# Two of three weight sums of a seven-product unit on GpSimd instead of VectorE, and the work at four pass ends placed anew

## The reference

```python
h2 = rms_norm(x, norm2_g[l])
ff = jnp.square(jax.nn.relu(h2 @ w_ff1[l]))      # 256 x 8192
x = x + ff @ w_ff2[l]                            # 8192 x 2048, the "down" product
return rms_norm(x, final_g)                      # then the third block, built alike:
x = x + jnp.square(jax.nn.relu(h @ w_up[l])) @ w_down[l]
return rmsnorm(x, norm_final_g)
```

## Time and profile before

| | |
|---|---|
| median of 3 runs | 3254.99 us (3254.61 to 3255.85) |
| profiled execution, own time | 3254.65 us |
| its span | 3252.9 us |
| TensorE busy | 3223.1 us, 99% |
| VectorE busy | 2388.0 us, 73% |
| ScalarE busy | 1593.2 us, 49% |
| GpSimd busy | 350.9 us, 11% |
| granted TensorE clock | 0.999 of full speed |

### The profile page before, as it was taken

One profiled execution on the slowest core, in us unless ns is written; L12 is line 12 of the kernel. 1 busy time (PEld: TensorE's weight loads), 2 busy tenths in 40 slices (PEclk: granted clock), 3 DMA queues, 4 the chain that ended last, 5 costly groups with the idle time before them and its releaser, 6 DMA issues.

```text
span 3252.9 us, 51117 instructions
## 1 busy us (share of the span) xinstructions
PE 3223.1 (99%) x20707; PEld 2777.6 (85%) x20707; DVE 2388.0 (73%) x3219; ACT 1593.2 (49%) x2153; POOL 350.9 (11%) x348
## 2 busy tenths in 40 slices
PE   9999999999999999999999999999999999999999
PEld 8888888888878888888888888877888888888887
DVE  6468666567487667776778877788778777877787
ACT  5354434444553456445445544555455545544455
POOL 3000233300102003311100000011010100000010
PEclk9999999999999999999999999999999999999999
DMA  8455443447546557655665566555655555565664
GB/s 254 148 183 181 140 140 125 141 158 234 189 145 199 171 174 223 184 178 186 188 188 190 198 201 188 184 180 194 188 172 171 182 182 188 201 207 187 200 206 170
DMA packets 508960, 595.04 MB, mean 183 GB/s; under 512 B 25429, under 2 KB 418485, under 8 KB 508214
## 3 DMA queue, kind: packets, MB, share of 16 engines
q1 hardware_dynamic: 508582, 591.51, 57.1%
q10 hardware_dynamic: 144, 0.26, 0.0%
HBM read 585.32 MB, written 6.32 MB: 182 GB/s over the span
## 4 chain that ended last, share of the span: by engine, by line
PE 95%; DVE 3%; ACT 1%; issue 1%; POOL 1%; DMA 0%; SPq 0%; POOLq 0%; ACTq 0%; DVEq 0%
PE gp L3217 42%; PE gp L3221 22%; PE gp L3082 12%; PE gp L3088 6%; PE sidep L1346 3%; PE sidep L3107 3%; PE gp L3107 2%; PE sidep L3112 1%; PE gp L3112 1%; DVE w_parts L3003 1%; POOL stage L717 0%; PE sidep L1645 0%; ACT w_parts L2991 0%; PE sidep L1649 0%; DVE x_parts L671 0%
## 5 line engine op out<-in xcount | busy, mean ns | idle before, releaser
L3003 DVE TENSOR_TENSOR w_parts<-ring,w_parts 128x1024 fp32r<-128x1024 f32 x988 | 1242.4, 1278 | 145.3 <-ACT w_parts L2991 143.0
L3217 PE MATMUL gp<-x_parts,w_parts 128*128 128x512 f32 x5264 | 1296.7, 394 | 0.0
L2991 ACT ACTIVATE w_parts<-ring 128x1024 fp32r<-128x1024 f32 x988 | 1010.2, 1052 | 239.9 <-PE gp L3088 114.8
L3217 PEld LDWEIGHTS gp<-x_parts,w_parts 128*128 128x128 f32 x5264 | 958.9, 188 | 186.1 <-issue 2.5
L3221 PEld LDWEIGHTS gp<-x_parts,w_parts 128*128 128x128 f32 x5264 | 684.2, 191 | 34.5 <-issue 2.5
L3221 PE MATMUL gp<-x_parts,w_parts 128*128 128x256 f32 x5264 | 706.4, 284 | 0.4 <-DVE w_parts L3003 0.4
L2347 ACT ACTIVATE lo_half<-gp 128x512 f32<-128x512 f32 x204 | 122.0, 598 | 654.8 <-PE gp L3217 520.1
L3082 PE MATMUL gp<-w_parts,ff_parts 128*128 128x512 f32 x1280 | 342.8, 390 | 0.0
L3082 PEld LDWEIGHTS gp<-w_parts,ff_parts 128*128 128x128 f32 x1280 | 239.8, 188 | 49.5
L2514 DVE TENSOR_TENSOR stage<-gp,lo_half 128x512 f32<-128x512 f32 x152 | 104.8, 690 | 237.8 <-ACT lo_half L2347 235.8
L3088 PE MATMUL gp<-w_parts,ff_parts 128*128 128x512 f32 x640 | 197.1, 389 | 0.0
(11 more groups left out here) (467 smaller groups left out, 3121.9 us busy)
## 6 DMA issues: line engine op xcount, KB each, us to landing
ring<-w_in SPq DMA_DIRECT2D x440, 512.0 KB, 4.3
ring<-w_ff SPq DMA_DIRECT2D x256, 512.0 KB, 4.6
ring<-w_up SPq DMA_DIRECT2D x128, 512.0 KB, 3.9
ring<-w_down SPq DMA_DIRECT2D x128, 512.0 KB, 4.9
ring<-w_out SPq DMA_DIRECT2D x96, 512.0 KB, 4.1
ring<-w_branch_attn SPq DMA_DIRECT2D x16, 512.0 KB, 4.3
ring<-w_branch_rwkv SPq DMA_DIRECT2D x16, 512.0 KB, 5.0
gate_scratch<-stage SPq DMA_DIRECT2D x16, 256.0 KB, 2.2
```

Of the source, the lines that this page charges most:

```text
L2991: act.activation(w_parts[:, q % PARTS, 0], ring[:, u % RING, SLOT * half:SLOT * half + SLOT, :], ACT.Copy).then_inc(high_split, 1)
L3003: v.tensor_tensor(w_parts[:, q % PARTS, 1], ring[:, u % RING, SLOT * half:SLOT * half + SLOT, :], w_parts[:, q % PARTS, 0].bitcast(F32), A ...
L3217: return pe.matmul(gp[:, k % 2, j, :, :], w_parts[:, q % PARTS, 0, c, j * P:(j + 1) * P], operand(s, b, SLOT * n + c), start=(n == 0 and c ...
```

## The change

`combine_weights` keeps `t13` on VectorE. The two instructions of `t24` go to a new function of GpSimd, called at the same distance ahead (q + 4), with the same waits. In VectorE's stream `t13` waits in addition until GpSimd has finished the sums of the unit before.

Beside it, at the ends of the passes of `down2_1`: ScalarE makes the high parts of two blocks together one slot after the pass half ends, and the squares of the second of them two slots after those of the first; GpSimd's additions of the squares stand at the same places; the low parts of the first four blocks go from the pass end into the next pass, 12, 18, 24 and 36 slots in; and the norm's steps come later (sums on TensorE 6.34 instead of 5.67 slots after the section, the root 6.67 instead of 6.0).

```diff
-        def turned_high(act, s, n):
-            norm, gain, _ = next_norm[s.name]
-            act.wait_ge(finished, fin_count(s.name, n))
-            for c in (2 * n, 2 * n + 1):
-                m = act.activation(x_parts[:, c, 0, :], xt[:, c, :], ACT.Copy, scale=gains(gain, c))
-            m.then_inc(x_high_split, 1)
-            norm.square(act, n, xt[:, 2 * n:2 * n + 2, :], lambda i: par("final2", 2 * n + i))
+        def turned_high(act, s, b):
+            for n in (2 * b, 2 * b + 1):
+                act.wait_ge(finished, fin_count(s.name, n))
+                for c in (2 * n, 2 * n + 1):
+                    m = act.activation(x_parts[:, c, 0, :], xt[:, c, :], ACT.Copy, scale=gains(next_norm[s.name][1], c))
+                m.then_inc(x_high_split, 1)
+        def turned_squares(act, s, n):
+            next_norm[s.name][0].square(act, n, xt[:, 2 * n:2 * n + 2, :], lambda i: par("final2", 2 * n + i))
...
-            return norm.thread(gain, S[name].end, (2.67, 2.67, 4.0, 4.0) if sets == 1 else (5.67, 6.0, 7.0, 7.34))
+            return norm.thread(gain, S[name].end, (2.67, 2.67, 4.0, 4.0) if sets == 1 else (6.34, 6.67, 7.34, 7.67))
...
         def combine_weights(v, q):
-            if q >= n_slots or seven_step(q) not in (1, 2):
+            if q >= n_slots or seven_step(q) != 1:
                 return
...
+            if steps:
+                v.wait_ge(weights_combined, steps)
             v.tensor_tensor(t13, tiles[:, 2:4], tiles[:, 0:3:2], ALU.subtract).then_inc(weights_combined, 1)
-            else:
-                if n > s.first_seven + 2 or b:
-                    v.wait_ge(low_split, seven_units[seven_units.index(q - 2) - 1] + 3)
-                v.wait_ge(weights_combined, steps + 1)
-                v.tensor_tensor(t24[:, 0], t13[:, 1], tiles[:, 0], ALU.add).then_inc(weights_combined, 1)
-                v.wait_ge(weights_combined, steps + 2)
-                v.tensor_tensor(t24[:, 1], tiles[:, 1], t24[:, 0], ALU.subtract).then_inc(weights_combined, 1)
+        def combine_more_weights(pool, q):
+            if q >= n_slots or seven_step(q) != 2:
+                return
...
+            if n > s.first_seven + 2 or b:
+                pool.wait_ge(low_split, seven_units[seven_units.index(q - 2) - 1] + 3)
+            pool.wait_ge(weights_combined, steps + 1)
+            pool.tensor_tensor(t24[:, 0], t13[:, 1], tiles[:, 0], ALU.add).then_inc(weights_combined, 1)
+            pool.wait_ge(weights_combined, steps + 2)
+            pool.tensor_tensor(t24[:, 1], tiles[:, 1], t24[:, 0], ALU.subtract).then_inc(weights_combined, 1)
...
@@ GpSimd's loop
-                    for late in (1, 2):
-                        if turned_block(q, late) and turned_block(q, late)[0].name in next_norm:
-                            next_norm[turned_block(q, late)[0].name][0].add(pool, 2 * turned_block(q, late)[1] + late - 1)
+                    for i in range(2):
+                        if normed_block(q, 1 + 2 * i):
+                            s, b = normed_block(q, 1 + 2 * i)
+                            next_norm[s.name][0].add(pool, 2 * b + i)
                     side.run(q)
+                    combine_more_weights(pool, q + 4)
@@ ScalarE's loop
-                    for late in (1, 2):
-                        if turned_block(q, late) and turned_block(q, late)[0].name in next_norm:
-                            turned_high(act, turned_block(q, late)[0], 2 * turned_block(q, late)[1] + late - 1)
+                    if normed_block(q, 1):
+                        turned_high(act, *normed_block(q, 1))
+                    for i in range(2):
+                        if normed_block(q, 1 + 2 * i):
+                            s, b = normed_block(q, 1 + 2 * i)
+                            turned_squares(act, s, 2 * b + i)
@@ VectorE's loop
-                    for late in (2, 3):
-                        if turned_block(q, late) and turned_block(q, late)[0].name in next_norm:
-                            turned_low(v, turned_block(q, late)[0], 2 * turned_block(q, late)[1] + late - 2)
+                    for i in range(2):
+                        if normed_block(q, 2 + i) and normed_block(q, 2 + i)[1] >= 2:
+                            s, b = normed_block(q, 2 + i)
+                            turned_low(v, s, 2 * b + i)
+                    for n, at_slot in enumerate((12, 18, 24, 36)):
+                        if q == S["down2_1"].slot0 + S["down2_1"].slots + at_slot:
+                            turned_low(v, S["down2_1"], n)
```

More of the change, by code:

```diff
@@ L2925, in combine_weights @@
             tiles, (t13, t24) = weight_tiles(unit_of[q]), combined_weights(s)
-            if seven_step(q) == 1:
-                wait_loaded(v, q, 0)
-                wait_loaded(v, q, 1)
-                if n > s.first_seven + 1 or b:
-                    v.wait_ge(low_split, seven_units[seven_units.index(q - 1) - 1] + 2)
-                else:
-                    v.wait_ge(ff_split, up_count(s.hidden, 15))
-                    v.wait_ge(slot_used, s.slot0)
-                if n == s.first_seven + 1 and b and s.name.startswith("down3"):
-                    v.wait_ge(rows_added, row_base(s, b) - 2)
-                v.tensor_tensor(t13, tiles[:, 2:4], tiles[:, 0:3:2], ALU.subtract).then_inc(weights_combined, 1)
-            else:
-                if n > s.first_seven + 2 or b:
-                    v.wait_ge(low_split, seven_units[seven_units.index(q - 2) - 1] + 3)
-                v.wait_ge(weights_combined, steps + 1)
-                v.tensor_tensor(t24[:, 0], t13[:, 1], tiles[:, 0], ALU.add).then_inc(weights_combined, 1)
-                v.wait_ge(weights_combined, steps + 2)
-                v.tensor_tensor(t24[:, 1], tiles[:, 1], t24[:, 0], ALU.subtract).then_inc(weights_combined, 1)
@@ new lines, in combine_weights @@
+            wait_loaded(v, q, 0)
+            wait_loaded(v, q, 1)
+            if n > s.first_seven + 1 or b:
+                v.wait_ge(low_split, seven_units[seven_units.index(q - 1) - 1] + 2)
+            else:
+                v.wait_ge(ff_split, up_count(s.hidden, 15))
+                v.wait_ge(slot_used, s.slot0)
+            if n == s.first_seven + 1 and b and s.name.startswith("down3"):
+                v.wait_ge(rows_added, row_base(s, b) - 2)
+            if steps:
+                v.wait_ge(weights_combined, steps)
@@ new lines, in combine_weights @@
+            v.tensor_tensor(t13, tiles[:, 2:4], tiles[:, 0:3:2], ALU.subtract).then_inc(weights_combined, 1)
+        def combine_more_weights(pool, q):
+            if q >= n_slots or seven_step(q) != 2:
+                return
+            s, b, n = where[q]
+            steps = WEIGHT_STEPS * seven_units.index(q - seven_step(q))
+            tiles, (t13, t24) = weight_tiles(unit_of[q]), combined_weights(s)
+            if n > s.first_seven + 2 or b:
[4 more added lines that the diff above has]
+            pool.tensor_tensor(t24[:, 1], tiles[:, 1], t24[:, 0], ALU.subtract).then_inc(weights_combined, 1)
@@ L3027, in turned_block, with normed_block @@
             return block if block and block[0].name.startswith("down2") else None
+        def normed_block(q, late):
+            block = turned_block(q, late)
+            return block if block and block[0].name in next_norm else None
         calm = ('qk1', 'za', 'rkv', 'branch', 'out', 'ga2', 'gb2', 'out2', 'up2_0', 'down2_0', 'up2_1', 'down2_1', 'u3', 'qk3_1',
```

## The result

The changed kernel takes **3271.91 us** (median of 4 runs, 3270.57 to 3272.09), the kernel before 3254.88 beside it. The ratio is 1.0050, with a 95% interval of 1.0038 to 1.0062: slower by 17.0 us. Forecast were 3262 us, and a range that ended at 3270.

A forecast was written before the change was run, and what follows sets the result against it. TensorE, busy 3223.1 of 3252.9 us, was taken as the bound. Terms +8.0 (mixed stages) - 1.6 + 1.6 - 0.8 = +7.2 us on 3254.65 gave 3261.9, predicted as 3262 us, range 3251 to 3270.

The forecast's parts named there:

- seven like passes, sixth unit: Sixth unit of seven passes: holds make the second slot's low part late, TensorE stands 0.9 us each, 6.3 us in all.
- second pass of `down2_1`, third to fifth unit (but for its last slot): These units run later but within their margins of 2.7 us, so no loss.
- the same, fifth unit's last slot and sixth unit: Second pass of `down2_1`: low parts of x just before the fifth unit add 0.8 us to the sixth unit's wait: 1.7 us.
- wait at the first turn: First pass end of `down2_1`: TensorE's 2.87 us wait for plain sums falls to some 1.3 us: -1.6 (-2.8 to -0.5).
- unit behind it: Unit after the first pass end of `down2_1`: TensorE waits 4.9 instead of 3.3 us, +1.6 (-1.5 to +3).
- second pass end: Second pass end of `down2_1`: 3.0 us wait stays about as long, norm's wait 1.2 falls to 0.7: -0.8 (0 to -1.5).
- the holds of 1.10 us: Mixed stages: each `t24` sum on GpSimd takes 1.10 us of VectorE's time instead of 0.67, if VectorE has work waiting.
- strict turns at GpSimd's first sum: Mixed stages: VectorE and GpSimd alternate, each whole instruction at a time, and whichever already waits goes first.
- the rule of the Trainium skill that I weighed: VectorE with two SBUF inputs and GpSimd reading SBUF exclude each other; holds of 1.28 us would add 3 us.
- rival 3: Each sixth unit: GpSimd's second sum loses its turn or is slow, TensorE waits 2 us for `t24`'s rounding; 3270 us, chance 0.13.
- cost nothing: Units other than the sixth run 0.9 to 1.9 us later, within margins of 1.3 (first) and 2.7 us (rest): no loss.
- The one for GpSimd's root, which I had gone: Second pass end of `down2_1`: TensorE's small wait for the norm's root disappears, part of the -0.8 us.

The follow-up runs named there:

- the pause: Changed kernel, with VectorE waiting for the own end of each of the first four low parts of x in the second pass of `down2_1`: 3267.53 us.

## Why the prediction failed

It summed +7.2 us; the two profiles differ by 17.4.

| term | forecast | by the slots |
|---|---|---|
| seven like passes, sixth unit | +6.3 | +7.4 |
| second pass of `down2_1`, third to fifth unit (but for its last slot) | 0 | +4.0 |
| the same, fifth unit's last slot and sixth unit | +1.7 | +2.8 |
| wait at the first turn | -1.6 | -1.5 |
| unit behind it | +1.6 | +3.2 |
| second pass end | -0.8 | 0.0 |
| end of the last pass | 0 | +0.7 |
| ahead of the changed code (nearly all at 487 us) | 0 | +0.7 |

- **Right:** the holds of 1.10 us (the 512-column low part took 1.78 in place of 0.68), strict turns at GpSimd's first sum, but for three units of 48; 0.7 us of stand at L3127 per pass (0.9 forecast), stages of 51.5 us (51.4 forecast), VectorE busier with fewer instructions. By the rule of the Trainium skill that I weighed (SBUF — State Buffer, Who interferes with whom), the hold would have been GpSimd's whole 1.28 us; the trace has 1.10 again.
- **The step that failed:** "So the two alternate, each whole instruction at a time, and whichever already waits goes first." That holds only while VectorE's unbroken row of instructions consists of plain ones with two inputs. The low parts of x that the change puts at slots 12, 18 and 24 are scaled ones, and behind them GpSimd waits for three of VectorE's instructions in place of one. Here rival 3's mechanism (GpSimd's sum loses its turn, a rounding is late) was the right one, at three units of one pass in place of the sixth of each. (That its 3270 us lies nearer to the measured time than the forecast is chance: it came from 2 us in each of eight passes.) With it goes the statement that the other units "cost nothing". The slots show 4.0 us for it, and the pause, which restores the turns, takes 4.4 us off the time.
- **It could have been seen.** The trace of before has a GpSimd instruction that I did not look for, since I looked at the places that the change touches. VectorE and then GpSimd:

```profile
985.37 0.41 DVE L1765 MATCH_REPLACE8 low<-smalls,low 128x256 f32<-128x256 f32 x1
985.70 0.68 DVE L2514 TENSOR_TENSOR high<-gp,lo_half 128x512 f32<-128x512 f32 x1
986.30 4.62 DVE L3003 TENSOR_TENSOR w_parts<-ring,w_parts 128x1024 fp32r<-128x1024 f32 x4
```

```profile
986.47 5.60 POOL L2401 TENSOR_TENSOR high<-high,rstd 128x512 f32<-128x512 f32 x1 [2.25 <-DVE high L2514]
```

  Four low parts in 4.62 us, unhindered, and a sum that takes 1.28 us alone needs 5.60: no turns taken, in a row that began with comparisons.
- **Sized too small:** the sixth unit of the seven like passes (1.04 to 1.09 us, not 0.9) and that of the second pass of `down2_1` (2.8, not 1.7). With turns restored by the pause 2.8 us still go there, in three slots one behind the other (the fifth unit's last and the sixth's first two), where I had let only the sixth's second be late.
- **The unit behind the first turn:** the waits were forecast at 4.9 us and are 3.6: 2.9 for the rounding (3.2 forecast) and 0.7 for low parts (1.7 forecast). But I took a wait for its own length. Behind it the clock was at half for some 6.5 us, and the unit with the plain slots right behind it lost 3.2 in place of 1.6.
- **Second pass end:** the wait of 3.0 us stayed, as said, and the norm's wait fell from 1.2 to 0.8. The one for GpSimd's root, which I had gone, grew instead, from 0.3 us in the kernel before to 0.8, and took that back. Its row before:

```profile
PE sidep L599 <- POOL smalls L483: 0.3, 1, 0.3
```

- The +0.7 ahead of the changed code is there in some of the other kernels and missing in others, with and without sums on GpSimd; I take it for scatter. The +0.7 at the end (TensorE waits 0.45 us for a plain low part) comes with the sums on GpSimd and stays at 0.5 with the sixth units' sums on VectorE; I did not follow it further.

## What to carry to other kernels

GpSimd beside a full VectorE is paid twice, by the turns it takes (here 1.10 us of VectorE for 0.68 us of its work) and by those it does not get; so before moving work there, look for the slowest GpSimd instruction of that kind anywhere in the trace. If a chain runs through GpSimd, keep VectorE's row in front of its request to plain forms with two inputs, or put a pause of 0.03 us behind the others (here 1.5 us a unit); one plain instruction behind a scaled one did not help. Price a stand of TensorE with the clock that may fall behind it, and a stand removed with the next one that TensorE then meets.

## What the runs showed of the hardware

- Behind a scaled subtraction, a product, or a copy on VectorE (factors as number or column, one input or two), GpSimd did not get in between VectorE's next instructions with two SBUF inputs until VectorE paused, be it for 0.03 us; behind plain subtractions it got in behind the first. Why is open: the runs show when, not the mechanism. Open is too why a request made while such an instruction runs is served at once.
- The granted clock fell from 1.00 to 0.50 behind single stands of TensorE of 1.6 to 4.4 us, for some 3 to 7 us. The same stand did it in some kernels and not in others. At the second turn of `down2_1` TensorE stood for 3.0 us in twelve of the kernels: the clock fell behind it in six of them (3.01 to 3.04 us) and not in the other six (2.99 to 3.06 us), among these the kernel before and the changed one. What decides it is open. In the two places where its price was worked out above, one fall cost 2.2 and 2.7 us. With the first unit's sums on VectorE the one at the second turn came some 80 us behind the place of the edit.
